# Differential attention on one core: the value products as three fp32r products of split operands in place of one float32 product

## The reference, cut to what matters

```python
s = jnp.einsum('bqhcd,bkhcd->bhcqk', qb, k).astype(jnp.float32) * scale
s = jnp.where(mask, s, -jnp.inf)
p = jax.nn.softmax(s, axis=-1)
attn = p[:, :, 0] - lam_full * p[:, :, 1]
return jnp.einsum('bhqk,bkhe->bqhe', attn.astype(v.dtype), v)
```

## Time and profile before

| | before |
|---|---|
| median of 3 runs | 1343.63 us (1337.78 to 1344.31) |
| profiled execution | 1340.46 us, of which the span is 1338.7 us |
| PE busy | 1288.5 us (96%) |
| DVE, ACT, POOL busy | 777.7, 562.8, 610.8 us |
| value products, PE, line 1025 | 226 matmul records |
| attention steps | from 686.8 us to 904.8 us of the span |

### The profile page before, as it was taken

How to read it: one execution, slowest core, us unless ns; L and a number is a source line. 1 busy time by engine, 2 the same in 40 slices (tenths; PEclk the granted TensorE clock), 3 DMA queues, 4 the chain that set the end, 5 groups by cost and what they waited for, 6 DMA issues and landing times.

```text
span 1338.7 us, 26021 instructions
## 1 busy us (share of the span) xinstructions
PE 1288.5 (96%) x10235; PEld 1219.7 (91%) x10235; DVE 777.7 (58%) x994; ACT 562.8 (42%) x930; POOL 610.8 (46%) x351
## 2 busy tenths in 40 slices
PE   5899799999999999999999999989999999999998
PEld 4688699999999999999988989879999999998886
DVE  7788722258888888211335555563388888883002
ACT  5765334334343343222455566642334334342113
POOL 6322246643434444655564435425743444444441
PEclk9898899999999999999999999999999999999999
DMA  9222133222333332333322211212233333322221
GB/s 165 47 52 49 33 95 111 80 76 82 94 94 94 94 88 83 96 87 113 86 64 64 61 51 49 63 32 64 80 95 94 94 94 94 94 93 83 94 96 75
DMA packets 179546, 108.86 MB, mean 81 GB/s; under 512 B 7165, under 2 KB 173838, under 8 KB 179214
## 3 DMA queue, kind: packets, MB, share of 16 engines
q1 hardware_dynamic: 178885, 107.29, 28.8%
q10 hardware_dynamic: 592, 0.60, 0.2%
HBM read 101.58 MB, written 2.10 MB: 77 GB/s over the span
## 4 chain that ended last, share of the span: by engine, by line
PE 35%; issue 29%; DVE 13%; POOL 12%; ACT 2%; DVEq 1%; DMA 1%; POOLq 0%; ACTq 0%; SPq 0%
PE ps L869 9%; POOL wL L300 9%; PE ps L918 8%; PE ps L805 7%; DVE cv L1717 4%; DVE cv L1723 2%; PE ps L955 2%; PE ps L1025 1%; POOL acc L1938 1%; POOL sqt L1937 1%; PE ps L313 1%; DVE cg L1730 1%; DVE u L1712 1%; DVE u L1713 1%; ACT actH L1329 1%
## 5 line engine op out<-in xcount | busy, mean ns | idle before, releaser
L300 POOL TENSOR_TENSOR wL<-raw,wH 128x1024 fp32r<-128x1024 f32 x182 | 446.1, 2463 | 572.2 <-ACT wH L296 570.1
L313 PE MATMUL ps<-hgH,wH 128*128 128x264 f32 (+1 forms) x1408 | 286.1, 284 | 3.1 <-DVE hgL L1680 3.1
L313 PE MATMUL ps<-hgH,wL 128*128 128x264 f32 (+1 forms) x1408 | 285.8, 284 | 0.0
L313 PE MATMUL ps<-hgL,wH 128*128 128x264 f32 (+1 forms) x1408 | 285.7, 284 | 0.0
L296 ACT ACTIVATE wH<-raw 128x1024 fp32r<-128x1024 f32 x182 | 186.4, 1048 | 228.4 <-PE ps L313 81.2
L313 PEld LDWEIGHTS ps<-hgH,wH 128*128 128x128 f32 x1408 | 219.5, 189 | 3.6 <-issue 3.5
L313 PEld LDWEIGHTS ps<-hgL,wH 128*128 128x128 f32 x1408 | 219.1, 189 | 0.0
L313 PEld LDWEIGHTS ps<-hgH,wL 128*128 128x128 f32 x1408 | 218.4, 189 | 0.0
L1327 ACT ACTIVATE cg<-cg 128x528 f32<-128x528 f32 (+1 forms) x44 | 28.2, 640 | 267.9 <-DVE cg L1723 267.9
L1717 DVE TENSOR_SCALAR cv<-u,PV 128x528 f32<-128x528 f32 (+1 forms) x44 | 111.3, 2530 | 0.0
L1723 DVE SCALAR_TENSOR_TENSOR cg<-u,PV,cg 128x528 f32<-128x528 f32 (+1 forms) x88 | 99.2, 1127 | 13.0 <-DVE cv L1717 6.7
(11 more groups left out here) (303 smaller groups left out, 2449.1 us busy)
## 6 DMA issues: line engine op xcount, KB each, us to landing
raw<-ffn_w_up SPq DMA_DIRECT2D x88, 512.0 KB, 3.8
raw<-ffn_w_down SPq DMA_DIRECT2D x38, 512.0 KB, 3.4
raw<-attn_w_qkv SPq DMA_DIRECT2D x24, 512.0 KB, 3.7
raw<-s_w_glu SPq DMA_DIRECT2D x16, 512.0 KB, 3.8
TT<-KD SPq DMA_DIRECT2D x64, 64.0 KB, 2.4
raw<-attn_w_o SPq DMA_DIRECT2D x8, 512.0 KB, 4.1
raw<-ffn_w_down SPq DMA_DIRECT2D x8, 384.0 KB, 3.5
xb<-x SPq DMA_DIRECT2D x8, 256.0 KB
```

The source lines that it names most:

```text
L300: nc.gpsimd.tensor_tensor(wL[:, slot, 0:nk], raw[:, slot % 2, 0:nk], wH[:, slot, 0:nk].bitcast(F32), ALU.subtract).then_inc(w_lo, 1)
L313: mm = nc.tensor.matmul(ps[:, bank + b, 0:tw], w[:, slot, k, :], x[:, kt, t0:t0 + tw], start=first and k == 0 and s0, stop=last and k == n ...
```

## The change

The product `AT * vtok` becomes `ATH * vH + ATH * vL + ATL * vH`, all fp32r, in one PSUM group. DVE writes `ATH` (rounded copy of the probabilities) and then `ATL` (the rest, PSUM minus `ATH`); between the two it waits for its own semaphore `at_hi`. ACT's `v_out` writes `vH`, and a new `value_rest` on DVE writes `vL` from the same PSUM bank; `v_set`, which PE waits for, now comes from DVE. `vH` and `vL` hold two heads (index h % 2), so `v_out(h)` waits for the last value product of head h - 2. `V0` of the extra step is split likewise. Queue positions: `value_rest(h + 1)` stands at the end of DVE's step i = 3, `value_rest(0)` between `norm_v(0)` and `maxima(0)`.

```diff
-        vtok = at("vtok", [P, NT, D], F32, offset=O_VTOK)
-        O_OT = O_VTOK + NT * D
+        vH = at("vH", [P, 2, NT, P], F32R, offset=O_VTOK)
+        vL = at("vL", [P, 2, NT, P], F32R, offset=O_VTOK + 2 * NT * P)
+        O_OT = O_VTOK + 4 * NT * P
...
-                    values = V0[:, :] if i == NQ else vtok[:, t, h * P:(h + 1) * P]
-                    mm = nc.tensor.matmul(out_at(i), AT[:, t, :], values, start=t == 0, stop=t == n_tiles(i) - 1)
+                    hi, lo = (V0H[:, :], V0L[:, :]) if i == NQ else (vH[:, h % 2, t], vL[:, h % 2, t])
+                    nc.tensor.matmul(out_at(i), ATH[:, t, :], hi, start=t == 0, stop=False)
+                    nc.tensor.matmul(out_at(i), ATH[:, t, :], lo, start=False, stop=False)
+                    mm = nc.tensor.matmul(out_at(i), ATL[:, t, :], hi, start=False, stop=t == n_tiles(i) - 1)
...
+                if h >= 2:
+                    act.wait_ge(o_ps, step_of(h - 2, NQ - 1) + 1)
-                nc.scalar.activation(vtok[:, 1:NT, o], ps[:, b].rearrange("p (t c) -> p t c", c=P), ACT.Copy)
-                ins = nc.scalar.activation(vtok[0:META, 0:1, o], ps[0:META, b + 1:b + 2, 0:P], ACT.Copy)
+                nc.scalar.activation(vH[:, h % 2, 1:NT], ps[:, b].rearrange("p (t c) -> p t c", c=P), ACT.Copy)
+                ins = nc.scalar.activation(vH[0:META, h % 2, 0:1], ps[0:META, b + 1:b + 2, 0:P], ACT.Copy)
...
-                ins.then_inc(v_set, 1)
+                ins.then_inc(v_hi, 1)
...
+            def value_rest(h):
+                dve.wait_ge(v_hi, h + 1)
+                b = unit_bank(3 * h + 2)
+                V.tensor_tensor(vL[:, h % 2, 1:NT], ps[:, b].rearrange("p (t c) -> p t c", c=P),
+                                vH[:, h % 2, 1:NT].bitcast(F32), ALU.subtract)
+                ins = V.tensor_tensor(vL[0:META, h % 2, 0], ps[0:META, b + 1, 0:P], vH[0:META, h % 2, 0].bitcast(F32),
+                                      ALU.subtract)
+                if h == HEADS - 1:
+                    ins = V.tensor_tensor(V0L[:, :], ps[:, b + 1, P:2 * P], V0H[:, :].bitcast(F32), ALU.subtract)
+                ins.then_inc(v_set, 1)
...
-                V.tensor_copy(AT[:, 0:n_tiles(i)], probs_at(i).rearrange("p (t q) -> p t q", q=P)).then_inc(at_set, 1)
+                probs = probs_at(i).rearrange("p (t q) -> p t q", q=P)
+                V.tensor_copy(ATH[:, 0:n_tiles(i)], probs).then_inc(at_hi, 1)
+                dve.wait_ge(at_hi, n + 1)
+                V.tensor_tensor(ATL[:, 0:n_tiles(i)], probs, ATH[:, 0:n_tiles(i)].bitcast(F32), ALU.subtract).then_inc(at_set, 1)
...
+                if i == 3 and more:
+                    value_rest(h + 1)
...
                 norm_v(0)
+                value_rest(0)
                 maxima(0)
...
-                V.memset(vtok[:, 0], 0.0).then_inc(v_zero, 1)
+                V.memset(vL[:, :, 0].bitcast(F32), 0.0)
+                V.memset(vH[:, :, 0].bitcast(F32), 0.0).then_inc(v_zero, 1)
```

More of the change, by code:

```diff
@@ L205, in build @@
         Ab = att("Ab", [P, L])
-        AT = att("AT", [P, NT, P])
+        ATH = att("ATH", [P, NT, P], F32R)
+        ATL = att("ATL", [P, NT, P], F32R)
         Ob = att("Ob", [P, 2, NQ + 1, P])
@@ L209, in build @@
         v0T = att("v0T", [P, HEADS, META])
-        V0 = att("V0", [P, P])
+        V0H = att("V0H", [P, P], F32R)
+        V0L = att("V0L", [P, P], F32R)
         mask0 = att("mask0", [P, P])
@@ L484, in build @@
         v_set = sem("v_set")
+        v_hi = sem("v_hi")
+        at_hi = sem("at_hi")
         v_zero = sem("v_zero")
@@ L1120, in _ @@
         def _(act):
-            for s in (v_set,):
-                act.sem_inc(s, FREE)
             for i, name in enumerate(("s5_a_re", "s5_a_im")):
@@ L1375, in v_out @@
                 b = unit_bank(3 * h + 2)
-                o = slice(h * P, (h + 1) * P)
                 if h == 0:
                     act.wait_ge(v_zero, 1)
-                nc.scalar.activation(vtok[:, 1:NT, o], ps[:, b].rearrange("p (t c) -> p t c", c=P), ACT.Copy)
-                ins = nc.scalar.activation(vtok[0:META, 0:1, o], ps[0:META, b + 1:b + 2, 0:P], ACT.Copy)
+                if h >= 2:
+                    act.wait_ge(o_ps, step_of(h - 2, NQ - 1) + 1)
+                nc.scalar.activation(vH[:, h % 2, 1:NT], ps[:, b].rearrange("p (t c) -> p t c", c=P), ACT.Copy)
+                ins = nc.scalar.activation(vH[0:META, h % 2, 0:1], ps[0:META, b + 1:b + 2, 0:P], ACT.Copy)
                 if h == HEADS - 1:
-                    ins = nc.scalar.activation(V0[:, :], ps[:, b + 1, P:2 * P], ACT.Copy)
-                ins.then_inc(v_set, 1)
+                    ins = nc.scalar.activation(V0H[:, :], ps[:, b + 1, P:2 * P], ACT.Copy)
+                ins.then_inc(v_hi, 1)
             def exponentials(n):
@@ L1484, in cmul @@
                 lk(e.tensor_tensor(o[1], t[2], t[3], ALU.add))
-            for s in (glu_free, *up_free, *h_new, qk_set, v_norm, o_lo):
+            for s in (glu_free, *up_free, *h_new, qk_set, v_norm, v_set, o_lo):
                 dve.sem_inc(s, FREE)
```

## The result

| | before | after |
|---|---|---|
| median of 6 runs | 1341.91 us (1337.78 to 1344.31) | 1363.81 us (1358.45 to 1365.54) |
| profiled execution: span | 1338.7 us | 1361.7 us |
| ratio after / before | | 1.0158, 95% interval 1.0132 to 1.0185 |

The change makes the kernel slower by 1.58%, 21 us (18 to 25 by the interval). The forecast was 15.4 us. First the page of the changed kernel, part 1, and the busy times in stretches that answer to the earlier trace rows; the last stretch is wider, and I come back to its granted clock (the number after the five engines).

The account below looks back on a forecast made before the run. PE was taken to bound the kernel in steps 0 to 26, DVE also in steps 27 to 32. 10.4 + 0.1 (before step 0) + 4.9 = 15.4 us slower gave 1357 us, range 1350 to 1365.

Parts of the forecast that it names:

- DVE or the clock takes more: Rival: rests over 1.25 us in steps i = 2, a longer tail or lower clock; 11 more, 1368 us; chance 0.11.
- 2 for the clock: Allowance of 2 us in the range's high end, for added idle stretches in the last head lowering the granted clock.
- 3 for the tail: Allowance of 3 us for the tail, added to the sum in the range's high end.
- PE's product, 0.112 more for each tile: On PE, three fp32r products at 0.112 us replace a float32 product of 0.223, for each of 113 tile products.
- slow stream: Rival: narrow fp32r streams at four cycles a column, 0.417 more for each of 113, about 1389 us; chance 0.04.
- hidden loads: Rival: weight loads are hidden and a product costs its stream, 0.058 us; about 1340 us; chance 0.04.
- Only PE counts: Rival: DVE's tail terms are mostly covered; 11 to 13.4 us more, about 1353.5 us; chance 0.09.
- Steps 0 to 26: Attention before the tail: DVE's extra work is hidden, 93 products lie fully on PE's path, 10.4 us.
- The tightest is i = 2: In steps 0 to 26, least slack between DVE's copy and PE's products: 1.25 us against 0.73 for the rest, so hidden.
- The last head, 4.9: Steps 27 to 32, also at DVE's pace: 0.87 + 0.92 + 0.73 + 0.27 + 0.56 + 0.73 + 0.84 = 4.9 us.
- step 27: Last head: `ATL` lengthens the chain copy, difference, norm that PE waits for, in place of its own five products; +0.87 us.
- What would show it: Signs: 339 records 0.111 to 0.112 apart, a head about 1.57 us longer; PE idle in steps 0 to 26 means wrong.

Follow-up runs that it names:

- e1: The changed kernel with POOL's weight-rest subtraction waiting for DVE's head norm: 1358.56 us, 1.0137 of the kernel before.
- e2: The changed kernel with three products per tile, all of high parts, without `value_rest` and `ATL`: 1351.28 us, 1.0082 of the kernel before.
- e5: The e1 kernel with the float32 product of before in the extra step and the last head: 1351.33 us, 1.0077 of the kernel before.
- e3: The changed kernel without the product of high probabilities and value rests, all rests still made: 1347.02 us, 1.0057 of the kernel before.
- e4: The changed kernel with the split parts in bf16 in place of fp32r: 1340.76 us, 1.0009 of the kernel before.
- e6: The e5 kernel with bf16 in place of fp32r parts for heads 0 to 6: 1337.89 us, 0.9975 of the kernel before.
- e7: The e3 kernel with DVE's head norm of heads 0 to 5 waiting until POOL has begun its subtraction: 1354.23 us, 1.0100 of the kernel before.

## Why the prediction was right or wrong

The direction and the price of a product were right, and most of the last head. The time lies inside the range, near its upper end; the ratio forecast, 1.0115, is under the measured interval. The loss itself, 21 to 23 us, is above the 13.4 to 17.5 that had most of the chance and lies towards the rival "DVE or the clock takes more". The range held because its upper end had 5 us of allowances on top of the sum, 2 for the clock and 3 for the tail; the largest missing term lay in neither, so that it held is partly luck. The rival named PE's wait in steps i = 2, but by a rest of over 1.25 us; the rest took 0.69 and came 0.04 behind the copy, as forecast. Point by point:

- **PE's product, 0.112 more for each tile: right.** e1 has A +10.0, e2 +10.5, e5 +9.6 against 89 * 0.112 = 10.0. That the load sets it is shown by e3 (two loads cost what float32 costs, and the first two starts are 0.06 apart) and e4 (bf16 loads of half the time, half the price). The rivals of a slow stream and of hidden loads fall by the same runs. "Only PE counts" falls by e2, 12 us over before, against the 22 of the change.
- **Steps 0 to 26, "The tightest is i = 2", "slack 1.25 against 0.73": this step failed.** The slack was counted from a copy that stays where it was. But DVE's work ahead of the copy moved: `Ob` of step i = 1 waits for the longer products, and 0.33 us were enough to put the head norm from 0.13 ahead of POOL's subtraction to 0.19 behind it. The collision costs DVE 2.0 us, and 2.0 and the rest's 0.73 together overran the slack: 0.79 in each of six steps, 4.7 us, where the sum had nothing. Alone they do little: the collision without the rest cost 0.1 a step (e2), the rest without the collision nothing (e1, e3). The terms of the sum were each priced with the others at rest.
- **The last head, 4.9: near in the sum, wrong in one step.** In B the forecast has 0.45 for the products of step 26, then 0.87, 0.92, 0.73, 0.27, 0.56, 0.73 and 0.87 up to the first product of step 32: 5.4. Measured 5.76, of which 0.8 is step 26's collision and about 0.25 the half clock in step 32 (five transposes took 1.01 in place of 0.76), so 4.7. The difference is step 27, which gave 0.17 in place of 0.87; each of the other terms is within 0.15 of its forecast. There the prediction put DVE's rest wholly into the chain copy, difference, norm, and missed that this chain was already held by POOL. Before:

```profile
878.21 2.37 POOL L300 TENSOR_TENSOR wL<-raw,wH 128x1024 fp32r<-128x1024 f32 x1 [3.43 <-ACT wH L296]
...
878.81 1.93 DVE L1782 SCALAR_TENSOR_TENSOR Ab<-Pb,tiny 128x128 f32<-128x128 f32 x1
```

`difference(28)` ended at 880.74, 0.16 behind the subtraction (880.58). After the change `ATL` starts it 0.85 us later, it takes 1.25 (893.85 to 895.10) and again ends 0.15 behind POOL (894.95): the rest filled time in which DVE would have waited.
- **The clock, an allowance of 2: too small, by all that is known.** The changed kernel has 56 us at half clock in both of its sessions, before 43 and 51 in those of the experiments; only the 51 was taken beside a run of the changed kernel. At up to 0.5 us for each (0.46 in e6) that makes 2.5 us, and 6 against the 43. 10.4 + 4.7 + 4.2 = 19.3, and the 2 to 4 that are left up to 21 to 23 are of that size. In the first profile 4.5 us of the loss lie behind B, where the forecast has nothing; 14.6 of its 17 us at half clock are there, and 3.4 in the one of before. In this table runs with added waits in the last head have 52 to 56 us, those without 46 to 49. That suggests the waits as the cause, but e6's profile speaks against it, and the two sessions of before, 43 and 51 without such waits, differ by as much. What starts those stretches stays open.
- **What would show it:** PE idle in steps 0 to 26 was named as a sign of error, and it was one: a head is 2.35 us longer from step 4 to step 8, not 1.57. The 339 records and their distance of 0.112 came as forecast.

## What to carry to other kernels

When an instruction gets longer, look not only at who waits for it, but at who starts next to whom afterwards: a shift of 0.3 us changed which of DVE and POOL came first, and that cost more than the shift. Look for such pairs in the profile of the kernel as it is: the same instruction at two very different times, with no wait shown, or a small form slower than a larger one of its line. Where a term is added to a chain, look whether the chain has a wait in it that the profile does not show as one. Before splitting a small float32 product into three, count weight loads, not columns: at 128 columns an fp32r product cost its load here, so three cost one and a half times the float32 product's two, and bf16, with a shorter load, gained. In the last head, where the filling work ran out, nearly every instruction added to the feeding engine lay on the path; a change can be kept out of such a part.

## What the runs showed of the hardware

- A DVE tensor_tensor with both inputs in SBUF and a POOL tensor_tensor of 1024 columns hold each other up: 0.69 alone, 2.70 to 2.75 started 0.2 us behind POOL's 2.38 (the change), 2.63 at 0.29 behind (e7); POOL takes 2.82 when DVE has begun 0.13 ahead. DVE's scalar_tensor_tensor of two SBUF tensors (`difference`) is held too: 0.37 alone at 144 columns, 1.21 to 1.24 started 1.3 behind POOL (before). DVE instructions that read PSUM and one SBUF tensor were not lengthened (`ATL` 0.69 for 512 columns at 763.74 in e1, beside POOL's subtraction).
- Starts of back-to-back matmuls of 128 columns: 0.111 to 0.112 us in fp32r, 0.055 in bf16, with loads of 0.20 and 0.10; the first two of a group of fp32r ones, 0.06 (e3).
- 6.8 us at half clock cost PE 3.1 us (e6).
